# Gate matrices from three bfloat16 matmuls per token instead of one float32 matmul

## The chip, the cores and the metric

One core of a Trainium2 chip runs one step of a decoder layer for a prompt group (512 tokens) and a sample group (8 sequences of 4 tokens). The metric is the device time of one execution in microseconds. Runs of this kernel agree within about 0.5%.

## The reference, cut to what matters

The change lies in the last part of the layer, PEER: each token picks, for each of 8 heads, the 16 best of 128 x 128 one-neuron experts, and adds their outputs, weighted by a gate.

```
s1, i1 = lax.top_k(s[:, :, 0], PEER_TOPK)
s2, i2 = lax.top_k(s[:, :, 1], PEER_TOPK)
cand = (s1[..., :, None] + s2[..., None, :]).reshape(...)
cidx = (i1[..., :, None] * PEER_NKEYS + i2[..., None, :]).reshape(...)
top, pos = lax.top_k(cand, PEER_TOPK)
eidx = jnp.take_along_axis(cidx, pos, axis=-1)
gate = jax.nn.softmax(top, axis=-1)
a = jnp.einsum('thkd,td->thk', u_tab[eidx], xb).astype(jnp.float32)
act = (jax.nn.gelu(a) * gate).astype(xb.dtype)
return jnp.einsum('thk,thkd->td', act, v_tab[eidx])
```

An expert has a first index (0 to 127) and a second one (0 to 127). A token has 128 picks (8 heads of 16).

## The kernel before, in words

The first 384 prompt tokens are computed densely: all 128 x 128 experts for each token. The table of the first layer of experts, `u`, comes in 128 tiles of 128 experts x 1024; the second table, `v`, in another 128 tiles. Each tile is split into a rounded part `tHi` (ScalarE, `t_hi`) and a rest `tLo` (GpSimd, `lo_part`), and `product(n)` on TensorE is 24 matmuls of 128 x 384 over the tile and the split activations. The other tokens (the last 128 of the prompt and the 32 samples) are computed sparsely: `gather(q)` on GpSimd starts an indirect DMA of 128 rows of the table, and VectorE forms a dot product (`dot`, later `row_add`) against the activations in PSUM (`h_rows`).

The dense way needs, for each token, a 128 x 128 matrix of gates: zero but at the token's picks. It is built by TensorE as a product of two one-hot matrices. For one token, partition p is one of the 128 picks; `oh2` holds 1 where the second index of the pick is the column, `oh1` holds 1 where the first index is, and `w1` is `oh1` times the gate of the pick. `oh2` transposed times `w1` is the gate matrix. All are float32.

Work is cut into 48 steps of 8 tokens. `one_hots(st)` on VectorE (L1726) makes the matrices of a step by three instructions of 128 x 1024; `gate_product(st)` on TensorE (L926) multiplies them in two parts of four tokens, each part into one PSUM bank; ScalarE copies each part out to `stage` (L1251) and stores it to DRAM. Two buffers hold `oh2` and `w1`, so VectorE may be one step and a bit ahead: `one_hots(st)` waits for the products of step st - 2. The iota of the keys (`iota_p`) and the gates (`g_cols`) lie in PSUM, the indices (`idx12`) and `oh1` in SBUF.

The order on each engine is written out by hand. The 48 steps are laid over 62 table tiles, n = 51 to 112 (`gate_steps`): TensorE runs product(n) and behind it, for 48 of the 62, one gate_product. VectorE runs for each step `one_hots` and then two `dot`s. GpSimd runs `lo_part(n)` and then the gathers that are due (two for a step). ScalarE runs for each n the gelu of the product, `t_hi(n + 3)`, the store, and the two copies of a gate step. The stretch ahead of it on VectorE (L1694 to L1718) is the retrieval of the picks, four passes of `retrieve`, beside products 0 to 50 on TensorE.

Of the kernel before, what the change touches and what calls it, by code (L numbers as in the profile page):

```python
# [7 lines left out]
BF16 = mybir.dt.bfloat16  # L8
U32 = mybir.dt.uint32
ALU = mybir.AluOpType  # L10
# [3 lines left out]
P = 128  # L14
# [12 lines left out]
PH, PK = 8, 16  # L27
# [29 lines left out]
TD = T - P - TS  # L57
STILES = [TD, 0, 128, 256]
NST = len(STILES)
# [3 lines left out]
STEP_TOK = TB // 4  # L63
# [11 lines left out]
GATE_BANKS = (4, 5, 7)  # L75
# [60 lines left out]
def build(nc, a, o):  # L136
    with ExitStack() as ctx:
# [3 lines left out]
        def at(name, shape, offset, dt=F32):  # L141
            n = 4
            for s in shape[1:]:
                n *= s
            assert base <= offset and offset + n <= top and offset % 32 == 0, (name, offset, n)
            return nc.alloc_sbuf_tensor_at(name, shape, dt, offset=offset)
# [18 lines left out]
        iota = keep("iota", [P, P])  # L165
# [7 lines left out]
        pos_sq = pos[0]  # L173
# [11 lines left out]
        SPL_AT = TAB_AT + 32768  # L185
# [68 lines left out]
        at_ = TAIL + 6 * 2176 + 256  # L254
# [24 lines left out]
        tLo = at("tLo", [P, SPL, KT, P], TAB_AT + 16384, F32R)  # L279
        ug = at("ug", [P, UG, D], SPL_AT)  # L280
        ga = [at(f"ga{i}", [P, TD], (SPL_AT + 24576, SPL_AT + 24576 + 4 * TD, pos_sq + 6528)[i]) for i in range(3)]
        idx12 = at("idx12", [P, 2, TD], SPL_AT + 27648)
        a_s = at("a_s", [P, NDOT], SPL_AT + 30720)
        act_s = at("act_s", [P, NDOT], SPL_AT + 31360)
        eidx = at("eidx", [P, NDOT], SPL_AT + 32000, U32)
# [3 lines left out]
        zp = [Z_AT]  # L289

        def peer(name, shape, dt=F32):
            n = 4
            for q in shape[1:]:
                n *= q
            t = at(name, shape, zp[0], dt)
            zp[0] += -(-n // 32) * 32
            assert zp[0] <= C_AT + 26400, name
            return t
# [16 lines left out]

        zp[0] = Z_AT
        stage = peer("stage", [P, 2, NKEY, TB])
        oh2 = peer("oh2", [P, 2, STEP_TOK, P])
        w1 = peer("w1", [P, 2, STEP_TOK, P])
        oh1 = at("oh1", [P, STEP_TOK, P], pos_sq + 1024)  # L320

        zp[0] = Z_AT
        actHi0 = peer("actHi0", [P, GRP, TD], F32R)
# [14 lines left out]
        ps = ctx.enter_context(nc.psum_tensor("ps", [P, 8, 512], F32))  # L338
# [10 lines left out]

        flat = ps[:].rearrange("p b n -> p (b n)")  # L350
        h_rows = flat[:, 2 * 512:4 * 512]
        g_cols = flat[:, 6 * 512:6 * 512 + TD]
        iota_p = flat[:, 6 * 512 + TD:7 * 512]
        y_rows = h_rows

        def late_bank(n):
# [101 lines left out]
        s_oh = sem("one_hots_ready")  # L458
# [36 lines left out]
        def over(ap, n):  # L495

            return ap.unsqueeze(len(ap.shape)).broadcast_to(list(ap.shape) + [n])
# [171 lines left out]
        def _(pe):  # L669
            mm = nc.tensor.matmul  # L670
# [80 lines left out]
            for n in range(1, U_CONV):  # L751
# [7 lines left out]
                if n == 13:  # L759
# [5 lines left out]
                    for w, src in enumerate((row_r, row_li)):  # L765
                        for i in range(NH + 1):
                            m = P if i < NH else TS
                            c = 160 + (w * (NH + 1) + i) * NH
                            last = nc.tensor.transpose(ps[0:m, 6, c:c + NH], src[0:NH, i * P:i * P + m], ident[0:NH, 0:NH])
# [39 lines left out]
            for h in range(NH):  # L809
# [27 lines left out]
                for i in range(NH):  # L837
                    mm(ps[:, 6, i * P:TP], vtok[:, i, :], er[:, EOFF[i]:EOFF[i] + TP - i * P],
                       start=(i == 0), stop=(i == NH - 1))
                pe.wait_ge(s_c0, 16 * (h + 1))  # L840
                pe.wait_ge(s_qn, 1)
                for b in range(NB):
                    mm(ps[:, 2, 256 + b * NL:256 + (b + 1) * NL], csb[:, b, :], qwi[:, h, b * NL:(b + 1) * NL],
                       start=(b == 0), stop=False)
# [4 lines left out]
                for i in range(NH):  # L849
                    mm(ps[0:GR, 7, i * P:TP], dsel[:, h, :], er[:, EOFF[i]:EOFF[i] + TP - i * P],  # L850
                       start=(h == 0 and i == 0), stop=(h == NH - 1 and i == NH - 1))
# [74 lines left out]
            def gate_product(st):  # L926

                pe.wait_ge(s_oh, st + 1)
                for part in range(2):
                    i = 2 * st + part  # L930
                    if i >= len(GATE_BANKS):
                        pe.wait_ge(s_gev, i - len(GATE_BANKS) + 1)
                    for t in range(4):
                        last = mm(ps[:, GATE_BANKS[i % 3], t * P:(t + 1) * P], oh2[:, st % 2, 4 * part + t, :],  # L934
                                  w1[:, st % 2, 4 * part + t, :], start=True, stop=True)
                    last.then_inc(s_gmm, 1)

            for n in range(NCH):
# [6 lines left out]
                if n == N_SHUF:  # L945
                    pe.wait_ge(s_best, 1)
                    for q in range(3):
                        for i in range(1, NST):
                            last = nc.tensor.transpose(ps[:, 4 + q, (i - 1) * P:i * P], best[:, q, i, :], ident[:])
# [7 lines left out]
            for n in range(NCH, NT):  # L957
# [8 lines left out]
                if n == N_FOLD:  # L966
                    pe.wait_ge(s_yb, 1)
                    pe.wait_ge(s_flush, n - NCH - 1)
                    for k in range(KT):
                        last = mm(ps[:, late_bank(n + 2), k * TS:(k + 1) * TS], y_b[:, k * P:(k + 1) * P], fold[:],  # L970
                                  start=True, stop=True)
                    last.then_inc(s_fold, 1)
                if n == N_YT:
                    pe.wait_ge(s_yrow, 1)
                    for k in range(KT):
                        last = nc.tensor.transpose(y_rows[:, k * P:(k + 1) * P], ug[:, 0, k * P:(k + 1) * P], ident[:])
# [309 lines left out]
        def _(v):  # L1286
            link = linker(v, s_dch)
# [431 lines left out]
            v.wait_ge(s_bestT, 1)  # L1719
            for q in range(2):  # L1720
                nc.vector.tensor_copy(idx12[:, q], ps[:, 5 + q, 0:TD])
            link(nc.vector.tensor_copy(oh1[:, 0:4, :], ps[:, 4, :].rearrange("p (t c) -> p t c", c=P)))
            nc.vector.tensor_copy(iota_p, iota[:])
            link(nc.vector.tensor_copy(g_cols[:], oh1[:, 0:3, :].rearrange("p t c -> p (t c)")))

            def one_hots(st):  # L1726

                at_ = slice(STEP_TOK * st, STEP_TOK * (st + 1))
                keys_ = iota_p.unsqueeze(1).broadcast_to([P, STEP_TOK, P])
                if st >= 2:  # L1730
                    v.wait_ge(s_gmm, 2 * (st - 1))
                tt(oh2[:, st % 2], keys_, over(idx12[:, 1, at_], P), ALU.is_equal)
                if st:
                    v.wait_ge(s_oh, st)
                link(tt(oh1[:], keys_, over(idx12[:, 0, at_], P), ALU.is_equal))
                tt(w1[:, st % 2], oh1[:], over(g_cols[:, at_], P), ALU.mult).then_inc(s_oh, 1)

            for st in range(NSTEP):
                one_hots(st)
# [142 lines left out]
```

## Time and profile before

| what | us |
|---|---|
| median of 3 runs | 1723.83 (1715.46 to 1724.01) |
| the profiled execution, its own time | 1713.92 |
| its span, first to last instruction | 1712.2 |
| TensorE busy | 1670.4 (98%) |
| VectorE busy | 1183.7 (69%) |
| GpSimd busy | 1123.3 (66%) |
| ScalarE busy | 665.1 (39%) |
| granted TensorE clock, mean | 0.993 |

The span is the time from the first to the last instruction of the profiled execution. Durations are those of single instructions; neighbouring matmuls overlap in their pipeline, so the pace of a run of matmuls is read from the distance of their starts, not from their durations. The gate steps run from 750.7 us to 1089.3 us of the span.

### The profile page before, as it was taken

What the parts mean: (1) busy time and instruction counts of PE and PEld (TensorE: products, weight loads), DVE (VectorE), ACT (ScalarE), POOL (GpSimd) and SP (SyncE); (2) the same over time, 40 slices, a digit from 0 to 9 for tenths busy, and PEclk for the clock granted to TensorE, in tenths of its full rate; (3) what the DMA queues carried; (4) which work ended last, traced back from release to release, by engine and by line L of the source; (5) the groups of instructions that cost most, each with busy time, mean ns of one, the idle gap of its engine ahead of it and who ended that gap; (6) DMA issues with size and microseconds to landing.
All of it is one profiled execution on the core that took longest, in us unless ns stands there. A gap on an engine that the chain in (4) does not pass through costs nothing.

```text
span 1712.2 us, 27326 instructions
## 1 busy us (share of the span) xinstructions
PE 1670.4 (98%) x10559; PEld 1604.4 (94%) x10559; DVE 1183.7 (69%) x2324; ACT 665.1 (39%) x1059; POOL 1123.3 (66%) x677
## 2 busy tenths in 40 slices
PE   8999999899999999999999999999999999999996
PEld 3899878697999999999999999999999999999995
DVE  4340244645777899999787778446787888888755
ACT  2554222333334333343433433334444344444442
POOL 1767322132336888877766676778889799999952
PEclk9999999999999999999999999999999999999998
DMA  8645222044204999979999999979999999999951
GB/s 280 213 154 160 74 72 101 13 143 148 89 36 141 308 299 295 341 260 337 351 342 349 347 352 339 340 300 352 394 406 405 362 408 401 407 407 400 401 187 62
DMA packets 192705, 461.27 MB, mean 269 GB/s; under 512 B 21184, under 2 KB 99008, under 8 KB 192448
## 3 DMA queue, kind: packets, MB, share of 16 engines
q1 hardware_dynamic: 79872, 242.31, 40.3%
q0 software_dynamic: 46080, 167.79, 26.0%
q10 hardware_dynamic: 66624, 49.42, 8.7%
q8 instruction: 84, 1.38, 0.3%
q14 instruction: 45, 0.37, 0.1%
HBM read 407.64 MB, written 51.83 MB: 268 GB/s over the span
## 4 chain that ended last, share of the span: by engine, by line
PE 54%; DVE 4%; issue 1%; POOL 0%; DVEq 0%; ACT 0%
PE ps L923 49%; PE ps L934 5%; DVE ug L1575 1%; DVE yo L1821 0%; DVE eqb L1687 0%; DVE rs L1819 0%; DVE pick L1674 0%; DVE ps L1585 0%; POOL tLo L649 0%; DVE cand L1652 0%; DVE rs L1297 0%; PE ps L676 0%; DVE pos L1660 0%; DVE eqa L1678 0%; DVE pos L1651 0%
## 5 line engine op out<-in xcount | busy, mean ns | idle before, releaser
L649 POOL TENSOR_TENSOR tLo<-tab,tHi 128x1024 fp32r<-128x1024 f32 x256 | 621.4, 2428 | 163.5 <-ACT tHi L1174 160.6
L1174 ACT CAST tHi<-tab 128x1024 fp32r<-128x1024 f32 x256 | 268.1, 1047 | 288.0 <-PE ps L923 219.7
L923 PE MATMUL ps<-hHi,tLo 128*128 128x384 f32 x1024 | 352.1, 344 | 0.0
L923 PE MATMUL ps<-hHi,tHi 128*128 128x384 f32 x1024 | 345.7, 338 | 0.0
L923 PE MATMUL ps<-hLo,tHi 128*128 128x384 f32 x1024 | 344.9, 337 | 0.0
L923 PE MATMUL ps<-actHi,tLo 128*128 128x384 f32 x1024 | 342.5, 334 | 1.6 <-POOL tLo L649 1.6
L923 PE MATMUL ps<-actLo,tHi 128*128 128x384 f32 x1024 | 342.2, 334 | 0.0
L923 PE MATMUL ps<-actHi,tHi 128*128 128x384 f32 x1024 | 342.2, 334 | 0.0
L637 POOL TENSOR_TENSOR wLo<-raw,wHi 128x1024 fp32r<-128x1024 f32 x53 | 128.0, 2416 | 289.6 <-ACT wHi L1005 289.6
L1575 DVE SCALAR_TENSOR_TENSOR ug<-ug,ps 128x1024 f32<-128x1024 f32 x160 | 191.4, 1217 | 46.8 <-DMA ug<-in_urows,eidx 45.7
L1585 DVE SCALAR_TENSOR_TENSOR ps<-ug,act_s,ps 128x1024 f32<-128x1024 f32 x158 | 202.5, 1282 | 5.0
L923 PEld LDWEIGHTS ps<-actHi,tLo 128*128 128x128 f32 x1024 | 192.2, 188 | 2.1 <-issue 1.9
L923 PEld LDWEIGHTS ps<-hHi,tHi 128*128 128x128 f32 x1024 | 193.2, 189 | 0.0
L923 PEld LDWEIGHTS ps<-hHi,tLo 128*128 128x128 f32 x1024 | 193.2, 189 | 0.0
L923 PEld LDWEIGHTS ps<-hLo,tHi 128*128 128x128 f32 x1024 | 192.6, 188 | 0.0
L923 PEld LDWEIGHTS ps<-actHi,tHi 128*128 128x128 f32 x1024 | 192.2, 188 | 0.0
L923 PEld LDWEIGHTS ps<-actLo,tHi 128*128 128x128 f32 x1024 | 192.2, 188 | 0.0
L1235 ACT ACTIVATE ga<-ps 128x384 f32<-128x384 f32 x112 | 54.9, 490 | 351.5 <-PE ps L923 351.5
L693 PE MATMUL ps<-hHi,wLo 128*128 128x272 f32 x848 | 180.0, 294 | 7.4 <-DVEq L1460 2.8
L659 POOL DMA_INDIRECT ug<-in_urows,eidx x160 | 158.4, 990 | 38.1 <-issue 27.6
L659 POOL DMA_INDIRECT ug<-in_vrows,eidx x160 | 151.4, 947 | 43.3 <-issue 22.7
L693 PE MATMUL ps<-hLo,wHi 128*128 128x272 f32 x848 | 175.7, 289 | 0.0
(356 smaller groups left out, 2471.8 us busy)
## 6 DMA issues: line engine op xcount, KB each, us to landing
tab<-in_tab SPq DMA_DIRECT2D x256, 512.0 KB, 6.6
raw<-in_w SPq DMA_DIRECT2D x101, 512.0 KB, 4.2
gate_scratch<-stage ACTq DMA_DIRECT2D x48, 512.0 KB, 6.4
gt<-gate_scratch SPq DMA_DIRECT2D x32, 768.0 KB, 6.9
gelu_scratch<-ga ACTq DMA_DIRECT2D x112, 192.0 KB, 5.9
gin<-gelu_scratch SPq DMA_DIRECT2D x112, 192.0 KB, 9.6
ug<-in_urows,eidx POOLq DMA_INDIRECT x160, 6.8
ug<-in_vrows,eidx POOLq DMA_INDIRECT x160, 7.6
```

The lines of the kernel that those rows point to most:

```text
L637: pool.tensor_tensor(wLo[:, i % 2], raw[:, p % RAW], wHi[:, i % 2].bitcast(F32), ALU.subtract).then_inc(s_wlo, 1)
L649: pool.tensor_tensor(tLo[:, n % SPL], tab[:, n % TABS], tHi[:, n % SPL].bitcast(F32), ALU.subtract).then_inc(s_tlo, 1)
L659: pool.indirect_dma_start(ug[:, q % UG, :], None, a["urows"] if q < NDOT else a["vrows"], bass.IndirectOffsetOnAxis(ap=eidx[:, q % NDOT:q ...
L693: last = mm(pair(n)[:, h], w, x[:, k, h * HF:(h + 1) * HF], start=first, stop=end)
L923: last = mm(ps[:, bank, 0:TD], w, x[:, k, 0:TD], start=first, stop=end)
L934: last = mm(ps[:, GATE_BANKS[i % 3], t * P:(t + 1) * P], oh2[:, st % 2, 4 * part + t, :], w1[:, st % 2, 4 * part + t, :], start=True, stop ...
L1174: nc.scalar.copy(tHi[:, n % SPL], tab[:, n % TABS]).then_inc(s_thi, 1)
L1235: f(out, ps[:, n % 2, 0:TD], ACT.Gelu_apprx_tanh).then_inc(s_gelu, 1)
L1575: stt(ug[:, slot], ug[:, slot], 1.0, h_rows, ALU.mult, ALU.mult, accum_out=a_s[:, q:q + 1]).then_inc(s_item, 1)
L1585: stt(y_rows, ug[:, slot], act_s[:, k:k + 1], y_rows, ALU.mult, ALU.add).then_inc(s_item, 1)
```

## The change

The one-hots, the indices, the iota and the gates become bfloat16. An index up to 127 and a 0 or 1 are exact in bfloat16; a gate is split into three bfloat16 pieces (`gate3`: rounded, the rest rounded, the rest of that), and for each token three matmuls, one per piece, are added up in PSUM. The pieces are made once, ahead of the steps. In the tiles two tokens are interleaved: the last dimension is a pair of tokens, so an operand that repeats along the keys still has two neighbouring elements. TensorE reads one token of a pair, with a step of two elements. The iota (`key2`) and the gates no longer lie in PSUM: every operand of the step's VectorE instructions is in SBUF.

```diff
+        oh2 = at("oh2", [P, 2, STEP_TOK // 2, P, 2], zp[0], BF16)
+        w3 = at("w3", [P, 2, 3, STEP_TOK // 2, P, 2], zp[0] + 4096, BF16)
+        oh1 = at("oh1", [P, STEP_TOK // 2, P, 2], pos_sq + 512, BF16)
+        key2 = at("key2", [P, P, 2], pos_sq + 512 + 2048, BF16)
+        idx12 = at("idx12", [P, 2, TD], pos_sq + 512 + 4096, BF16)
...
-        g_cols = flat[:, 6 * 512:6 * 512 + TD]
-        iota_p = flat[:, 6 * 512 + TD:7 * 512]
...
                     for t in range(4):
-                        last = mm(ps[:, GATE_BANKS[i % 3], t * P:(t + 1) * P], oh2[:, st % 2, 4 * part + t, :],
-                                  w1[:, st % 2, 4 * part + t, :], start=True, stop=True)
+                        out, pair_, one = ps[:, GATE_BANKS[i % 3], t * P:(t + 1) * P], 2 * part + t // 2, t % 2
+                        keys_, pieces = oh2[:, st % 2, pair_, :, one], w3[:, st % 2, :, pair_, :, one]
+                        for piece in range(3):
+                            last = mm(out, keys_, pieces[:, piece], start=(piece == 0), stop=(piece == 2))
...
-            link(nc.vector.tensor_copy(oh1[:, 0:4, :], ps[:, 4, :].rearrange("p (t c) -> p t c", c=P)))
-            nc.vector.tensor_copy(iota_p, iota[:])
-            link(nc.vector.tensor_copy(g_cols[:], oh1[:, 0:3, :].rearrange("p t c -> p (t c)")))
+            nc.vector.tensor_copy(key2[:], over(iota[:], 2))
+            link(nc.vector.tensor_copy(gate3[:, 0], ps[:, 4, 0:TD]))
+            link(tt(gate_rest[:], ps[:, 4, 0:TD], gate3[:, 0], ALU.subtract))
+            link(nc.vector.tensor_copy(gate3[:, 1], gate_rest[:]))
+            link(tt(gate_rest[:], gate_rest[:], gate3[:, 1], ALU.subtract))
+            link(nc.vector.tensor_copy(gate3[:, 2], gate_rest[:]))
 
             def one_hots(st):
 
                 at_ = slice(STEP_TOK * st, STEP_TOK * (st + 1))
-                keys_ = iota_p.unsqueeze(1).broadcast_to([P, STEP_TOK, P])
+                keys_ = key2[:].unsqueeze(1).broadcast_to([P, STEP_TOK // 2, P, 2])
+
+                def along_keys(of_tokens):
+
+                    pairs_ = of_tokens.rearrange("p (q two) -> p q two", two=2)
+                    return pairs_.unsqueeze(2).broadcast_to([P, STEP_TOK // 2, P, 2])
+
                 if st >= 2:
                     v.wait_ge(s_gmm, 2 * (st - 1))
-                tt(oh2[:, st % 2], keys_, over(idx12[:, 1, at_], P), ALU.is_equal)
+                tt(oh2[:, st % 2], keys_, along_keys(idx12[:, 1, at_]), ALU.is_equal)
                 if st:
                     v.wait_ge(s_oh, st)
-                link(tt(oh1[:], keys_, over(idx12[:, 0, at_], P), ALU.is_equal))
-                tt(w1[:, st % 2], oh1[:], over(g_cols[:, at_], P), ALU.mult).then_inc(s_oh, 1)
+                link(tt(oh1[:], keys_, along_keys(idx12[:, 0, at_]), ALU.is_equal))
+                for piece in range(3):
+                    last = tt(w3[:, st % 2, piece], oh1[:], along_keys(gate3[:, piece, at_]), ALU.mult)
+                last.then_inc(s_oh, 1)
```

On VectorE, from the end of the retrieval to the first dots of the first step, this stands in the kernel before (`idx_137` is `idx12`, `oh_159` is `oh2`, `oh_161` is `oh1`, `w_160` is `w1`, `ps` is PSUM):

```order
L1721 COPY idx_137<-ps 128x384 x2
L1722 COPY oh_161<-ps 128x512
L1723 COPY ps<-iota 128x128
L1724 COPY ps<-oh_161 128x384
L1732 TENSOR_TENSOR oh_159<-ps,idx_137 128x1024
L1735 TENSOR_TENSOR oh_161<-ps,idx_137 128x1024
L1736 TENSOR_TENSOR w_160<-oh_161,ps 128x1024
L1575 SCALAR_TENSOR_TENSOR ug,a_s<-ug,ps 128x1024 x2
```

and this in the changed one (`key_163` is `key2`, `oh_160` is `oh2`, `oh_162` is `oh1`, `w_161` is `w3`, `gate_137` is `gate3`):

```order
L1725 CAST idx_164<-ps 128x384 x2
L1726 CAST key_163<-iota 128x256
L1727 CAST gate_137<-ps 128x384
L1728 TENSOR_TENSOR gate_rest<-ps,gate_137 128x384
L1729 CAST gate_137<-gate_rest 128x384
L1730 TENSOR_TENSOR gate_rest<-gate_rest,gate_137 128x384
L1731 CAST gate_137<-gate_rest 128x384
L1745 TENSOR_TENSOR oh_160<-key_163,idx_164 128x1024
L1748 TENSOR_TENSOR oh_162<-key_163,idx_164 128x1024
L1750 TENSOR_TENSOR w_161<-oh_162,gate_137 128x1024 x3
L1579 SCALAR_TENSOR_TENSOR ug,a_s<-ug,ps 128x1024 x2
```

The place of the dots is the same; ahead of the first step stand 8 small instructions where 5 stood, and in every step 5 instructions of 128 x 1024 where 3 stood. The three of before have one SBUF input each, the five have two.

On TensorE, behind product(51), one part of a gate step between matmuls of the products stands in the kernel before as

```order
L923 MATMUL ps<-hLo,tHi 128x384
L934 MATMUL ps<-w_160,oh_159 128x128 x8
L923 MATMUL ps<-hHi,tLo 128x384
```

and in the changed one as

```order
L925 MATMUL ps<-hLo,tHi 128x384
L939 MATMUL ps<-w_161,oh_160 128x128 x24
L925 MATMUL ps<-hHi,tLo 128x384
```

One row here is a whole step of 8 tokens: 8 matmuls before, 24 now, at the same place between the products. (The trace shows a float32 matmul as two records.) GpSimd's and ScalarE's orders are the same in both.

## Rows read from the trace of the kernel before

**Rows 1.** The page: busy time of the engines; the chain that ended last.

```profile
PE 1670.4 (98%) x10559; PEld 1604.4 (94%) x10559; DVE 1183.7 (69%) x2324; ACT 665.1 (39%) x1059; POOL 1123.3 (66%) x677
...
PE ps L923 49%; PE ps L934 5%; DVE ug L1575 1%; DVE yo L1821 0%; DVE eqb L1687 0%; DVE rs L1819 0%; DVE pick L1674 0%; DVE ps L1585 0%; POOL tLo L649 0%; DVE cand L1652 0%; DVE rs L1297 0%; PE ps L676 0%; DVE pos L1660 0%; DVE eqa L1678 0%; DVE pos L1651 0%
```

**Rows 2.** Windows inside the gate stage: busy us by engine, clock, DMA share, GB/s.

```profile
900.00:950.00 50.00, 50.00 (x327) 50.00 (x327) 40.11 (x48) 19.73 (x32) 34.42 (x23) 1.00 1.02 353
```

**Rows 3.** Line 934, the gate matmuls: durations min/median/max, starts; who waited for them.

```profile
L934 PE MATMUL ps<-w,oh x768: 271/275/377, 750.7 to 1089.3; 128*128 128x128 f32 x192
...
  DVE oh L1732: 46.4, 12
```

**Rows 4.** Timeline of TensorE, one gate step and one product: start, duration, engine, line.

```profile
901.94 1.93 PEld L934 LDWEIGHTS ps<-w,oh 128*128 128x128 f32 x16
...
903.78 0.19 PEld L923 LDWEIGHTS ps<-hHi,tLo 128*128 128x128 f32 x1
...
907.94 0.19 PEld L934 LDWEIGHTS ps<-w,oh 128*128 128x128 f32 x1
```

**Rows 5.** Timeline of TensorE: sixteen 128-column matmuls with one pass each, merged.

```profile
538.08 1.90 PE L911 MATMUL ps<-identR,h_b 128*128 128x128 f32 x16
```

**Rows 6.** Timeline of VectorE, one gate step: first one-hot, first dot, next step.

```profile
904.09 1.22 DVE L1732 TENSOR_TENSOR oh<-ps,idx 128x1024 f32<-128x1024 f32 x1 [4.18 <-PE ps L934]
...
907.62 1.21 DVE L1575 SCALAR_TENSOR_TENSOR ug<-ug,ps 128x1024 f32<-128x1024 f32 x1
...
910.09 1.22 DVE L1732 TENSOR_TENSOR oh<-ps,idx 128x1024 f32<-128x1024 f32 x1
```

**Rows 7.** Timeline of VectorE in the retrieval, instructions with two SBUF inputs.

```profile
716.99 3.27 DVE L1674 TENSOR_TENSOR pick<-pabf,pcut 128x128 bf16<-128x128 f32 x1
...
732.61 0.69 DVE L1687 TENSOR_TENSOR eqa<-eqa 128x1024 bf16<-128x1024 bf16 x1
733.22 0.69 DVE L1687 TENSOR_TENSOR eqb<-eqb 128x1024 bf16<-128x1024 bf16 x1
733.94 0.42 DVE L1687 TENSOR_TENSOR eqa<-eqa 128x512 bf16<-128x512 bf16 x1
```

**Rows 8.** Timeline of GpSimd around the first row of Rows 7.

```profile
716.57 1.00 POOL L659 DMA_INDIRECT ug<-in_urows,eidx  x1 [0.30 <-issue]
717.60 2.41 POOL L649 TENSOR_TENSOR tLo<-tab,tHi 128x1024 fp32r<-128x1024 f32 x1
```

**Rows 9.** VectorE groups, 537 to 750 us (retrieval): shapes, count, busy us, mean ns, idle.

```profile
L1682 DVE TENSOR_TENSOR eqa<-eqa,ixt 128x2048 bf16<-128x2048 bf16 x4 | 13.3, 3314 | 0.1
L1678 DVE TENSOR_TENSOR eqa<-ranks,pick 128x2048 bf16<-128x2048 bf16 x4 | 7.8, 1940 | 0.0
L1687 DVE TENSOR_TENSOR eqb<-eqb 128x256 bf16<-128x256 bf16 x5 | 7.2, 1432 | 0.0
L1674 DVE TENSOR_TENSOR pick<-pabf,pcut 128x128 bf16<-128x128 f32 x4 | 6.7, 1664 | 0.0
L1687 DVE TENSOR_TENSOR eqb<-eqb 128x512 bf16<-128x512 bf16 x4 | 6.1, 1522 | 0.0
L1687 DVE TENSOR_TENSOR eqa<-eqa 128x1024 bf16<-128x1024 bf16 x4 | 5.6, 1394 | 0.0
...
L1682 DVE TENSOR_TENSOR eqb<-eqb,ixt 128x2048 bf16<-128x2048 bf16 x4 | 4.8, 1211 | 0.0
...
L1687 DVE TENSOR_TENSOR eqa<-eqa 128x512 bf16<-128x512 bf16 x4 | 1.7, 424 | 0.1
...
L1687 DVE TENSOR_TENSOR eqa<-eqa 128x256 bf16<-128x256 bf16 x5 | 1.5, 292 | 0.2
```

**Rows 10.** Groups of the gate stage, 745 to 1095 us, same columns.

```profile
L649 POOL TENSOR_TENSOR tLo<-tab,tHi 128x1024 fp32r<-128x1024 f32 x62 | 149.1, 2405 | 85.3 <-ACT tHi L1174 85.2
L1575 DVE SCALAR_TENSOR_TENSOR ug<-ug,ps 128x1024 f32<-128x1024 f32 x98 | 116.7, 1216 | 13.8 <-DMA ug<-in_urows,eidx 13.6
...
L1721 DVE COPY idx<-ps 128x384 f32<-128x384 f32 x2 | 1.0, 552 | 1.3 <-PE ps L949 1.3
```

More of the change, by code:

```diff
@@ L281, in build @@
         ga = [at(f"ga{i}", [P, TD], (SPL_AT + 24576, SPL_AT + 24576 + 4 * TD, pos_sq + 6528)[i]) for i in range(3)]
-        idx12 = at("idx12", [P, 2, TD], SPL_AT + 27648)
+        gate3 = at("gate3", [P, 3, TD], SPL_AT + 27648, BF16)
         a_s = at("a_s", [P, NDOT], SPL_AT + 30720)
@@ L317, in build @@
         stage = peer("stage", [P, 2, NKEY, TB])
-        oh2 = peer("oh2", [P, 2, STEP_TOK, P])
-        w1 = peer("w1", [P, 2, STEP_TOK, P])
-        oh1 = at("oh1", [P, STEP_TOK, P], pos_sq + 1024)
+        gate_rest = at("gate_rest", [P, TD], zp[0])
+        oh2 = at("oh2", [P, 2, STEP_TOK // 2, P, 2], zp[0], BF16)
[3 more added lines that the diff above has]
+        idx12 = at("idx12", [P, 2, TD], pos_sq + 512 + 4096, BF16)
+        assert 512 + 4096 + 4 * TD <= 3 * NST * PH * PK * 4
         zp[0] = Z_AT
```

## The prediction

> **What bounds the kernel now.** I read the page first: TensorE is busy for 98% of the span, and the chain that ended last runs over it, 49% through the products of the tables and 5% through the gate matmuls [rows 1]. 5% of 1712.2 is 86 us: that is all that cheaper gate matmuls could give if nothing took their place. The windows of the gate stage show TensorE without a gap at full clock, while VectorE is busy for 40 us of 50 and GpSimd for 34 [rows 2]; the DMA share is already about 1, so I also ask below what transfers do. The rows on the gate line say how close VectorE is: it waited for TensorE 12 times in 48 steps, 46.4 us together [rows 3]; in the other steps it arrived about when it was needed. So the stage has one bound and a second engine right behind it, and each is costed for itself.
>
> **TensorE, per step.** The weight loads give the pace: a gate step of 8 tokens begins at 901.94, the next product at 903.78, the next gate step at 907.94 [rows 4]. A gate step is 1.84 us (88 us for 48), a product 4.16 us, that is 0.173 us for each of its 24 matmuls of 384 columns. The stage of 62 products and 48 gate steps is 62 x 4.16 + 48 x 1.84 = 346 us, so TensorE needs 7.21 us for each gate step with its share of products (62/48 = 1.29 products, 5.37 us).
>
> After, a step is 24 bfloat16 matmuls of 128 columns. The trace has none. From below: 128 columns at the products' pace per column, 0.173 x 128/384 = 0.058 us. From above: sixteen matmuls of 128 columns in one pass take 1.90 us from first start to last end, about 0.11 us from start to start once the last one's duration of 0.27 is taken off [rows 5]; their weights are 4-byte and are loaded anew for each, so they may be paced by the load. Bfloat16 weights are half as many bytes; I take 0.065, near the lower end, since the products' row is the one in which columns and not loads set the pace. The ends for 1152 matmuls are 67 and 127 us, the value 75: against 88 that is -21, +39 and -13 us. TensorE would then need 5.37 + 24 x 0.065 = 6.93 us for a step.
>
> The Trainium skill ("TensorE: Matmul & The Clock Gate", section "Back-to-back issue gap") gives about 81 ns for each load-and-matmul pair at 128 columns in a sustained stream. By that the matmuls would take 93 us and TensorE alone would be 5 us slower than before; no row here shows a bfloat16 pair.
>
> **VectorE, per step.** Before: three instructions from 904.09 to 907.62, 3.53 us, then two dots with their accumulator reads until 910.09, 2.47 us, in all 6.0 us [rows 6]. To this come waits for gathered rows, 13.6 us over the stage [rows 10], 0.28 a step. After: five bfloat16 instructions of 1024. In the retrieval such instructions start 0.61 us apart, and 0.72 where the chain is linked [rows 7]; four by 0.61 and one by 0.72 is 3.16 us. The operand that repeats along the keys changes slowly but its innermost two elements are neighbours; L1682, whose second operand repeats too with eight neighbours inside, takes 1.21 us for 2048 [rows 9], the same rate, so I take it for granted here. Alone the change of type gives 0.37 us a step back: three instructions became five. Sum: 3.16 + 2.47 + 0.28 = 5.91 us, below TensorE's 6.93.
>
> But all five now have both inputs in SBUF, where before one input of each lay in PSUM. The retrieval shows what such instructions meet. A 128-element subtraction started at 716.99 lasts 3.27 us [rows 7]; GpSimd was in a gather from 716.57 to 717.57 and in a `tLo` subtraction from 717.60 to 720.01, and VectorE's instruction ended 0.25 us behind that [rows 8]. The f32 one-hots of before, beside the same `tLo`, show nothing of the kind: 1.22 us each [rows 6]. I conclude that a VectorE instruction with two SBUF inputs stands still while GpSimd's subtraction runs.
>
> The Trainium skill ("SBUF — State Buffer", section "Who interferes with whom") says it as a rule: a VectorE instruction with two SBUF inputs contends with a GpSimd instruction that reads SBUF, and the later one waits for all of the other. By that rule VectorE becomes the bound of the stage; without it TensorE stays the bound and the sum is -13 us. The two rows at 717 us agree with it.
>
> The size, from the groups of the retrieval [rows 9], for one pass: the two of 2048 that stall, (3.31 - 1.21) + (1.94 - 1.21) = 2.8 us; 1024, 1.39 - 0.69 = 0.7; 512, 1.52 - 0.42 = 1.1; 256, (1.43 - 0.29) x 5/4 = 1.4; the 128 pick, 1.66 less about 0.27, 1.4. Together 7.5 us of standing on 7.9 us of work (four 2048 at 1.21, two each at 0.69, 0.42, 0.29, one at 0.27), 0.94 us per us. There a `tLo` came every 4.16 us. In the gate stage one comes 1.29 times a step; with a step of about 8 us that is every 6.2 us, so the ratio is 0.94 x 4.16/6.2 = 0.63, and 3.16 us of work stand for 2.0 us. Bounds: all of the 1.29 `tLo` of 2.41 us [rows 10] and half a microsecond for each of two gathers, 4.1 us; and nothing, if the dots, which read PSUM and can run beside GpSimd, happen to cover each `tLo`.
>
> A step is then 5.91 + 2.0 = 7.9 us on VectorE against 6.93 on TensorE: TensorE waits for the one-hots, the stage lasts 48 x 7.9 = 380 us, +33 us against 346. Queued behind a standing one-hot are the two dots and with them the slots of the gathers, but these have three steps of room. GpSimd in turn waits at most one VectorE instruction (0.6 us) for each of its own, and has 35% of the stage idle [rows 2]. DMA carries the same bytes in a longer stage, so its share of about 1 falls and costs nothing; it would matter only if the stage became shorter.
>
> **Ahead of the steps.** Five small instructions become eight, of about 0.55 us by the row of a 384 copy [rows 10]: some +2 us, with a link between most, less 0.4 us on the first three one-hots; one has two SBUF inputs and may stand. TensorE waits there already, so +2 us is on the path.
>
> **Sum.** +33 + 2 = +35 us on the profiled execution's 1713.9 us: 1749 us, with its span at 1747. That execution stands 10 us under the median of the three runs; half of this for where a new median will lie gives 1754 us.
>
> **The rivals.**
> (B) *TensorE stays the bound.* VectorE's standing is below 1.0 us a step, because the dots cover it. For it: dots and accumulator reads are 2.47 us, as long as one `tLo`. Against: in the retrieval dots lie between too, and the stalls came all the same. Then -13 + 2 = -11 us: 1703, with the same 5 us for the median 1708 (1700 if a matmul takes 0.058).
> (C) *The new matmuls are paced by their weight load*, 0.11 us each: TensorE needs 5.37 + 2.66 = 8.0 us a step and is at least level with VectorE: +39 + 2, 1760 us. For it: [rows 5]; against: half the bytes.
> (D) *The change doesn't do what it says on VectorE*: with only pairs inside, the instructions run at the float32 rate, 5 x 1.18 = 5.9 us, a step is 8.6 us without and 12 with standing (0.63 of 5.9 is 3.7): +67 to over +200 us. Against: L1682.
>
> **How the numbers follow.** A 0.60, B 0.20, C 0.12, D 0.08. A's own range is a standing of 1.2 to 3.1 us, steps of 7.1 to 9.0 us: -5 to +86, that is 1716 to 1807 us. The whole range takes in the upper half of B and leaves out most of D: 1706 to 1806. What a measurement can tell from no change is about 0.5%, 9 us. Faster: 0.15 of B and 0.07 at A's low end, 0.22. Same: 0.05 of B, 0.05 of A, 0.10. Slower: 0.48 of A, C and D, 0.68.
>
> **What would show it.** In the trace of the changed kernel: the five one-hot instructions with a mean well above 0.69 us and a maximum near 3 us, long ones ending just behind a `tLo`; TensorE idle ahead of the gate matmuls, released by the last product with the gates, about 1 us a step; the gate line's first to last start some 370 us apart instead of 339; matmul starts 0.06 to 0.07 us apart. Wrong would be: one-hots all at 0.69 us (no standing, B), TensorE without gaps and the matmuls at 0.11 (C), or a minimum of 1.2 us for the one-hots (D).

## The result, and the profile after

The changed kernel takes 1729.43 us (median of 14 runs, 1725.46 to 1738.45) against 1722.51 us of the kernel before (14 runs, 1715.16 to 1726.48, a spread of 0.7% where 0.5% is said above): a ratio of 1.0058, 95% interval 1.0038 to 1.0078. It is slower by about 10 us, or 0.6%. The forecast was slower by 30. Its profiled execution took 1736.84 us with a span of 1735.1 us, 22.9 us more than the span of before; about half of that lies ahead of all that was changed, as shown below.

On the page of the changed kernel, the engines and the chain:

```profile
PE 1664.7 (96%) x10943; PEld 1587.8 (92%) x10943; DVE 1264.5 (73%) x2423; ACT 668.6 (39%) x1059; POOL 1144.0 (66%) x677
...
PE 34%; DVE 24%; issue 1%; POOL 0%; DVEq 0%; ACT 0%
PE ps L925 34%; DVE w L1750 7%; DVE ug L1579 7%; DVE oh L1745 5%; DVE oh L1748 2%; DVE yo L1836 0%; DVE eqb L1691 0%; DVE rs L1834 0%; DVE eqb L1686 0%; DVE ixt L1644 0%; DVE ps L1589 0%; DVE eqa L1682 0%; DVE pcut L1673 0%; POOL tLo L651 0%; DVE key L1726 0%
```

The gate matmuls are gone from the chain [rows 1]; in their place VectorE has 24% of it, with the one-hots (L1745, L1748, L1750) and the dots (L1579). A window of the gate stage, the counterpart of [rows 2], says the same: VectorE is full, TensorE no longer.

```profile
900.00:950.00 50.00, 47.12 (x368) 45.68 (x367) 49.79 (x58) 18.92 (x31) 38.26 (x23) 1.00 0.98 332
```

The gate line of the changed kernel: durations min/median/max, first and last start, and what TensorE waited for (us, times).

```profile
L939 PE MATMUL ps<-w,oh x1152: 217/218/308, 764.9 to 1111.9; 128*128 128x128 bf16 x192
its engine sat idle before it (us, times) until:
  DVE w L1750: 56.6, 41
```

and who waited for the products with the gates (L1750):

```profile
  PEld ps L939: 31.6, 26
  PE ps L939: 25.0, 15
```

From first to last start the stage lasts 347.0 us; in [rows 3] it is 1089.3 - 750.7 = 338.6 us. Before, VectorE waited for TensorE 12 times; now TensorE waits for VectorE. The 56.6 us and 41 times of the gate line are the waits of the weight loads (31.6, 26) and of the matmuls (25.0, 15) added up, and mostly the same waits seen twice: at 808.69 us a load waits for 1.75 us, and at 808.70 its matmul for 1.44. TensorE's matmuls are kept waiting 25 us in the stage, about 0.5 us a step.

The groups of the stage, 745 to 1110 us (busy us, mean ns; the 128 x 1024 instructions of VectorE, and GpSimd's two):

```profile
L651 POOL TENSOR_TENSOR tLo<-tab,tHi 128x1024 fp32r<-128x1024 f32 x63 | 155.9, 2474 | 72.5 <-ACT tHi L1178 71.6
L1750 DVE TENSOR_TENSOR w<-oh,gate 128x1024 bf16<-128x1024 bf16 x144 | 124.1, 917 | 1.7
L1579 DVE SCALAR_TENSOR_TENSOR ug<-ug,ps 128x1024 f32<-128x1024 f32 x96 | 113.0, 1213 | 0.0
L661 POOL DMA_INDIRECT ug<-in_urows,eidx x98 | 108.7, 1109 | 29.2 <-issue 15.0 <-DVE ug L1579 9.1
...
L1745 DVE TENSOR_TENSOR oh<-key,idx 128x1024 bf16<-128x1024 bf16 x48 | 90.9, 1893 | 0.0
...
L1748 DVE TENSOR_TENSOR oh<-key,idx 128x1024 bf16<-128x1024 bf16 x48 | 32.6, 679 | 0.0
```

Undisturbed, one of the five takes 0.68 us. Where nothing stands (`psum5` below) the same three groups have 90.4, 33.1 and 32.7 us busy; here they have 124.1, 90.9 and 32.6. The difference, 33.7 + 57.8 - 0.1 = 91.4 us, is 1.9 us of standing a step: time in which an instruction is held up. (My expectations below say 1.75; that came from subtracting single durations, which overlap by 0.07 us where instructions follow one another.) The dots wait for no gathered row any more (0.0, where [rows 10] has 13.6 us).

VectorE and GpSimd side by side, two steps and a half of the changed kernel (start, duration):

```profile
890.53 2.56 DVE L1745 TENSOR_TENSOR oh<-key,idx 128x1024 bf16<-128x1024 bf16 x1
...
895.54 1.21 DVE L1579 SCALAR_TENSOR_TENSOR ug<-ug,ps 128x1024 f32<-128x1024 f32 x1
...
897.82 0.92 DVE L1745 TENSOR_TENSOR oh<-key,idx 128x1024 bf16<-128x1024 bf16 x1
...
899.38 4.11 DVE L1750 TENSOR_TENSOR w<-oh,gate 128x1024 bf16<-128x1024 bf16 x3
...
905.69 2.94 DVE L1745 TENSOR_TENSOR oh<-key,idx 128x1024 bf16<-128x1024 bf16 x1
```

```profile
890.13 2.42 POOL L651 TENSOR_TENSOR tLo<-tab,tHi 128x1024 fp32r<-128x1024 f32 x1 [2.19 <-ACT tHi L1178]
...
895.79 2.41 POOL L651 TENSOR_TENSOR tLo<-tab,tHi 128x1024 fp32r<-128x1024 f32 x1 [0.56 <-ACT tHi L1178]
900.00 2.94 POOL L651 TENSOR_TENSOR tLo<-tab,tHi 128x1024 fp32r<-128x1024 f32 x1 [1.80 <-ACT tHi L1178]
...
905.67 2.42 POOL L651 TENSOR_TENSOR tLo<-tab,tHi 128x1024 fp32r<-128x1024 f32 x1
```

The one-hot that starts at 890.53 ends 0.54 us behind the subtraction that runs until 892.55, a little less than an undisturbed one needs. The subtraction of 895.79 falls on the two dots (895.54 to 897.82) and costs 0.2 us. That of 900.00 is itself stretched to 2.94 us by the running product and then holds the next for over 2 us; that of 905.67 starts just before the one-hot and costs it 2.3 us. Of the four subtractions here the dots cover one.

**Where the profiled execution's 22.9 us lie.** The transposes of the picks start at 743.4 us before and at 754.5 us after: 11.1 us come ahead of all that was changed. In a second profile of the kernel before (experiment 6) they start at 751.6 us, so 8.2 of the 11.1 us come without the change too. TensorE's wait for VectorE at the second turn to the sparse tokens, in the changed kernel's trace:

```profile
700.15 0.48 PE L913 MATMUL ps<-identR,hHi 128*128 128x128 f32 x1 [5.75 <-DVE ug L1579]
```

and in that of before:

```profile
692.29 0.33 PE L911 MATMUL ps<-identR,hHi 128*128 128x128 f32 x1 [0.58 <-DVE ug L1575]
```

Behind the long wait the granted clock is 0.56 in the ten microseconds from 700 (1.00 before), so the products there run for most of them at the lower of its two levels, 1.2 instead of 2.4 GHz. From the transposes to the first gate matmul it is 10.4 us instead of 7.3 (+3.1), the stage is +8.4, what follows it 623.2 instead of 622.9 (+0.3). 11.1 + 3.1 + 8.4 + 0.3 = 22.9. The part from the transposes on, where the change lies, is 11.8 us, which fits the ratio.

### The profile page after: what moved, and what is told of

Read it like the earlier page. It is cut to its first block, busy times and chain, and to the rows that moved or that the text cites. A ratio compares the mean times of both kernels' runs of the same rounds, so it can differ in the third digit from the quotient of the medians.

```text
span 1735.1 us, 28193 instructions
## 1 busy us (share of the span) xinstructions
PE 1664.7 (96%) x10943; PEld 1587.8 (92%) x10943; DVE 1264.5 (73%) x2423; ACT 668.6 (39%) x1059; POOL 1144.0 (66%) x677
## 4 chain that ended last, share of the span: by engine, by line
PE 34%; DVE 24%; issue 1%; POOL 0%; DVEq 0%; ACT 0%
PE ps L925 34%; DVE w L1750 7%; DVE ug L1579 7%; DVE oh L1745 5%; DVE oh L1748 2%; DVE yo L1836 0%; DVE eqb L1691 0%; DVE rs L1834 0%; DVE eqb L1686 0%; DVE ixt L1644 0%; DVE ps L1589 0%; DVE eqa L1682 0%; DVE pcut L1673 0%; POOL tLo L651 0%; DVE key L1726 0%
## 5 line engine op out<-in xcount | busy, mean ns | idle before, releaser
L1579 DVE SCALAR_TENSOR_TENSOR ug<-ug,ps 128x1024 f32<-128x1024 f32 x160 | 190.1, 1216 | 35.6 <-DMA ug<-in_urows,eidx 34.6
L661 POOL DMA_INDIRECT ug<-in_urows,eidx x160 | 174.4, 1090 | 44.1 <-issue 23.4
L695 PE MATMUL ps<-hHi,wHi 128*128 128x272 f32 x848 | 176.4, 289 | 0.0
```

The source lines that it names most:

```text
L661: pool.indirect_dma_start(ug[:, q % UG, :], None, a["urows"] if q < NDOT else a["vrows"], bass.IndirectOffsetOnAxis(ap=eidx[:, q % NDOT:q ...
L695: last = mm(pair(n)[:, h], w, x[:, k, h * HF:(h + 1) * HF], start=first, stop=end)
L1579: stt(ug[:, slot], ug[:, slot], 1.0, h_rows, ALU.mult, ALU.mult, accum_out=a_s[:, q:q + 1]).then_inc(s_item, 1)
```

## The experiments

The measure of each is the stage, first to last start of the gate matmuls (338.6 before, 347.0 after), and its ratio to the kernel before.

**1. GpSimd's subtraction cut short.**

```diff
+                q = slice(0, 8 if 53 <= n < 115 else P)
+                k = slice(0, 1 if 53 <= n < 115 else KT)
-            pool.tensor_tensor(tLo[:, n % SPL], tab[:, n % TABS], ...
+                pool.tensor_tensor(tLo[:, n % SPL, k, q], tab[:, n % TABS, k, q], ...
```

> The changed kernel with GpSimd's tLo subtraction cut from 128x1024 to 128x8 for tiles 53 to 114 (the rest of tLo is left as it was, so that part of the products is left out); gathers, DMAs and all waits stay. Theory (VectorE's one-hots stand still while GpSimd's subtraction holds the SBUF read they share): the five one-hot instructions fall from means of 1.9, 0.68 and 0.86 us to about 0.7 to 0.8, VectorE's step from 7.4 to about 5.9 us, TensorE becomes the bound, and the gate matmuls' first to last start takes about 322 us instead of 347 (61 products at 4.16 and 47 steps at 1.45). Rival 1 (the gathers hold it, not the subtraction): the one-hot means stay above 1.2 us and the stage near 345. Rival 2 (VectorE isn't the bound of the stage): one-hots get short, the stage stays at 347.

Its groups on VectorE, 745 to 1120 us, and its gate line:

```profile
L1752 DVE TENSOR_TENSOR w<-oh,gate 128x1024 bf16<-128x1024 bf16 x144 | 91.0, 686 | 1.6
L1747 DVE TENSOR_TENSOR oh<-key,idx 128x1024 bf16<-128x1024 bf16 x48 | 33.1, 690 | 46.8 <-PE ps L941 45.0
L1750 DVE TENSOR_TENSOR oh<-key,idx 128x1024 bf16<-128x1024 bf16 x48 | 33.1, 690 | 0.0
```

```profile
L941 PE MATMUL ps<-w,oh x1152: 217/218/233, 753.6 to 1075.7; 128*128 128x128 bf16 x192
```

No one-hot or product stands any more (the longest takes 0.694 us), VectorE waits for TensorE again, and the stage takes 322.1 us; 1700.11 us, ratio 0.9873 (0.9825 to 0.9921). The gathers were all there, so they don't hold a one-hot up: rival 1 is out, and with it the half microsecond for each gather in my upper bound.

**2. TensorE with one piece, VectorE with three.**

```diff
-                        for piece in range(3):
-                            last = mm(out, keys_, pieces[:, piece], start=(piece == 0), stop=(piece == 2))
+                        for piece in range(1):
+                            last = mm(out, keys_, pieces[:, piece], start=True, stop=True)
```

> The changed kernel with TensorE multiplying only the first of the three pieces (8 bfloat16 matmuls a step instead of 24; the other two pieces are left out of the product); VectorE makes all three as before. Theory (VectorE bounds the stage): first to last start of the gate matmuls stays at 345 to 350 us, and the 0.9 us that TensorE saves in each step comes back as idle time ahead of the gate matmuls (57 us becomes about 100). Rival (the matmul stream or TensorE's turn-round sets the pace): the stage shrinks by up to 47 x 0.92 = 43 us, to about 304.

```profile
L939 PE MATMUL ps<-w,oh x384: 217/218/308, 755.2 to 1113.9; 128*128 128x128 bf16 x192
its engine sat idle before it (us, times) until:
  DVE w L1750: 128.9, 57
```

With two thirds of the gate matmuls gone the stage is longer, 358.7 us; ratio 1.0098 (1.0060 to 1.0136). VectorE bounds it. (The 128.9 us count loads and matmuls again; the matmuls alone wait for 59.8 us.) That it grew by 12 us I had not expected. TensorE is idle for longer, and the clock that it is granted is 0.89 to 0.97 in the windows of 50 us from 800 us on, against 1.00 in the changed kernel. But VectorE is busy for 49.8 us of each 50 in both, so the lower clock doesn't lengthen the stage by itself; the 12 us are on VectorE. Its groups:

```profile
L1750 DVE TENSOR_TENSOR w<-oh,gate 128x1024 bf16<-128x1024 bf16 x144 | 155.5, 1134 | 1.7
...
L1745 DVE TENSOR_TENSOR oh<-key,idx 128x1024 bf16<-128x1024 bf16 x48 | 65.4, 1362 | 0.0
L1748 DVE TENSOR_TENSOR oh<-key,idx 128x1024 bf16<-128x1024 bf16 x48 | 39.2, 818 | 0.0
```

By the same subtraction 104 us of standing in place of 91, and now more of it in the products than in the first one-hot: the same subtractions of GpSimd fall on other instructions, and cost 2.2 us a step instead of 1.9.

**3. VectorE with one piece, TensorE with three products.**

```diff
-                            last = mm(out, keys_, pieces[:, piece], start=(piece == 0), stop=(piece == 2))
+                            last = mm(out, keys_, pieces[:, 0], start=(piece == 0), stop=(piece == 2))
...
-                for piece in range(3):
+                for piece in range(1):
                     last = tt(w3[:, st % 2, piece], ...
```

> The changed kernel with VectorE multiplying only the first piece of the gates (3 instructions of 128x1024 a step instead of 5); TensorE still runs 24 matmuls a step, all on that piece. Theory: VectorE's step falls to about 4.4 us and at most 1.2 us of standing, TensorE becomes the bound without gaps, the stage takes about 322 us (this is the case in which the change would have gained 16 us in the stage). Rival (bfloat16 matmuls with a step of two elements, or the copies out on ScalarE, hold the stage): it stays above 335 us.

```profile
L939 PE MATMUL ps<-w,oh x1152: 217/218/233, 754.4 to 1077.7; 128*128 128x128 bf16 x192
...
  issue: 7.2, 45
  DVE w L1750: 7.0, 5
```

The stage takes 323.3 us, ratio 0.9893 (0.9844 to 0.9942). All 1152 bfloat16 matmuls are there: on TensorE the change does what it is meant to. The standing missed its expectation: the two one-hots and the one product have 75.7, 62.0 and 35.7 us busy, by the same subtraction 1.6 us a step where at most 1.2 was expected. VectorE has room for it here, so the stage doesn't show it. Three such instructions stand for 1.6 us, five for 1.9.

**4. The kernel before, with both operands in SBUF.**

```diff
-                keys_ = iota_p.unsqueeze(1).broadcast_to([P, STEP_TOK, P])
+                keys_ = iota[:].unsqueeze(1).broadcast_to([P, STEP_TOK, P])
...
-                tt(w1[:, st % 2], oh1[:], over(g_cols[:, at_], P), ALU.mult).then_inc(s_oh, 1)
+                tt(w1[:, st % 2], oh1[:], over(g_sb[:, at_], P), ALU.mult).then_inc(s_oh, 1)
```

> The kernel before, float32 and one matmul per token, with the iota of the keys and the gates read from SBUF instead of PSUM: each of the three one-hot instructions has two SBUF inputs. Theory (the place of the operands, not the type, brings the standing): the three rise from 1.22 us to means between 1.4 and 2.4, VectorE's step from 6.0 to 7.3 to 7.8 us against TensorE's 7.21, the stage from 339 to between 343 and 365 us, the kernel 0.2 to 1.5% slower than before. Rival (the standing belongs to bfloat16 at the packed rate): all stays at 1.22 us and 339 us.

```profile
L1731 DVE TENSOR_TENSOR oh<-iota,idx 128x1024 f32<-128x1024 f32 x48 | 89.8, 1871 | 0.0
L1734 DVE TENSOR_TENSOR oh<-iota,idx 128x1024 f32<-128x1024 f32 x48 | 86.9, 1810 | 0.0
L1735 DVE TENSOR_TENSOR w<-oh,g_sb 128x1024 f32<-128x1024 f32 x47 | 86.8, 1846 | 1.6
```

```profile
L935 PE MATMUL ps<-w,oh x768: 271/275/422, 760.9 to 1123.6; 128*128 128x128 f32 x192
```

The three go from 1.22 us to 1.81 to 1.87, the stage from 338.6 to 362.7 us, ratio 1.0113 (1.0071 to 1.0156). The standing comes with the place of the operands and not with the type: 1.8 us a step here, with float32.

**5. Operands back in PSUM.** The pieces and the iota are made in SBUF and copied once to PSUM as 4-byte words, two bfloat16 each. `psum4` has room for the iota and two pieces:

```diff
+        in_ps = flat[:, 6 * 512:7 * 512].bitcast(BF16)
+        key_ps = in_ps[:, 0:2 * P].rearrange("p (k two) -> p k two", two=2)
+        gate_ps = in_ps[:, 2 * P:2 * P + 2 * TD].rearrange("p (g t) -> p g t", g=2)
...
-                    last = tt(w3[:, st % 2, piece], oh1[:], along_keys(gate3[:, piece, at_]), ALU.mult)
+                    last = tt(w3[:, st % 2, piece], oh1[:], along_keys(gate_ps[:, piece, at_] if piece < 2 else gate3[:, 2, at_]), ALU.mult)
```

> The changed kernel with the doubled iota and the first two gate pieces read from PSUM (copied there once, 4-byte words that hold two bfloat16 each), so that four of the five one-hot instructions of a step have one SBUF input; only the third product has two. Theory (two SBUF inputs are the cause): the four stand no longer (0.69 us), the fifth keeps a mean of 0.9 to 1.5 us; a step on VectorE needs about 6.1 us, TensorE bounds the stage, 322 to 326 us, the kernel 0.5 to 1.2% faster than before. Rival (bfloat16 from PSUM doesn't run at the packed rate): the four take 1.2 us each, a step 8 us, the stage over 380 us.

`psum5` also frees a gate bank for the rest:

```diff
-GATE_BANKS = (4, 5, 7)
+GATE_BANKS = (4, 5)
...
+        key_ps = ps[:, 7, 0:P].bitcast(BF16).rearrange("p (k two) -> p k two", two=2)
+        in_ps = flat[:, 6 * 512:7 * 512].bitcast(BF16)
+        rest_ps = ps[:, 7, P:P + 64].bitcast(BF16)
...
-                    last = tt(w3[:, st % 2, piece], oh1[:], along_keys(gate3[:, piece, at_]), ALU.mult)
+                    last = tt(w3[:, st % 2, piece], oh1[:], along_keys(gate_ps(piece, st)), ALU.mult)
```

> As psum4, but all five one-hot instructions read one operand from PSUM: the gate matmuls use two banks in turn instead of three, the third piece and the iota lie in the freed one; the doubled iota is also made ahead of the retrieval instead of right ahead of the steps. Theory: no standing in the stage, all five at 0.69 us, stage 322 us, and 2 us less ahead of it; 0.8 to 1.4% faster than before. Rival (three banks are needed, because the copies out on ScalarE come late): TensorE idles ahead of the gate matmuls for 0.5 us or more a step, the stage is 340 us or more.

Groups of `psum5`, 745 to 1090 us, and one gate step on TensorE's weight loads:

```profile
L663 POOL TENSOR_TENSOR tLo<-tab,tHi 128x1024 fp32r<-128x1024 f32 x64 | 154.5, 2413 | 71.2 <-ACT tHi L1190 71.1
...
L673 POOL DMA_INDIRECT ug<-in_urows,eidx x97 | 91.6, 944 | 28.8 <-issue 17.9 <-DVE ug L1591 7.2
L1766 DVE TENSOR_TENSOR w<-oh,ps 128x1024 bf16<-128x1024 bf16 x144 | 90.4, 683 | 1.7
...
L1761 DVE TENSOR_TENSOR oh<-ps,idx 128x1024 bf16<-128x1024 bf16 x48 | 33.1, 690 | 33.3 <-PE ps L951 33.2
L1764 DVE TENSOR_TENSOR oh<-ps,idx 128x1024 bf16<-128x1024 bf16 x48 | 32.7, 681 | 0.0
```

```profile
905.39 1.38 PEld L951 LDWEIGHTS ps<-w,oh 128*128 128x128 bf16 x24 [0.16 <-issue]
906.73 0.19 PEld L937 LDWEIGHTS ps<-hHi,tLo 128*128 128x128 f32 x1
```

With the full subtractions in place nothing stands, and bfloat16 from PSUM runs at the packed rate. The stage takes 323.7 us in `psum5` (754.0 to 1077.7) and 323.6 in `psum4` (763.8 to 1087.4), where the fifth instruction has a median of 0.685 us and a maximum of 1.88 us. Its mean is 0.77 us, below the 0.9 to 1.5 expected: one instruction with two SBUF inputs stands for 0.09 us a step, far less than a fifth of 1.9. Over all: `psum4` 1704.9 us, ratio 0.9931 (0.9904 to 0.9959); `psum5` 1706.0 us, 0.9921 (0.9899 to 0.9942). Both beat both kernels, by 0.7 to 0.8% the one before and by about 1.3% the changed one: the change pays once its operands are where the old ones were. Between the two no difference can be told. Two banks are enough: in `psum5` TensorE's loads idle 0.16 us ahead of a gate step, not the 0.5 of the rival. Ahead of the steps `psum5` takes 9.9 us from the transposes to the first gate matmul, 0.5 less than the changed kernel and not 2: three copies to PSUM were added, and a conversion of the gates stands there (1.12 us for 0.36).

**6. The iota made early; the kernel before once more.**

```diff
             nc.vector.tensor_copy(identR[:], ident[:]).then_inc(s_idr, 1)
+            nc.vector.tensor_copy(key2[:], over(iota[:], 2))
...
-            nc.vector.tensor_copy(key2[:], over(iota[:], 2))
             link(nc.vector.tensor_copy(gate3[:, 0], ps[:, 4, 0:TD]))
```

> The changed kernel with only one edit: the doubled iota is made ahead of the retrieval, so its 2.4 us conversion no longer stands between the transposed picks and the first one-hots. Theory: from the transposes to the first gate matmul 8.2 us instead of 10.4, TensorE's idle time there 4.9 to 2.7 us, stage unchanged at 345 to 350 us; in all 2 to 4 us less than the changed kernel, ratio to before 1.002 to 1.006. Rival (this wait costs nothing because VectorE bounds what follows anyway): the stage starts 2 us earlier but lasts 2 us longer.

The row that it takes away, in the changed kernel:

```profile
756.70 2.42 DVE L1726 CAST key<-iota 128x256 bf16<-128x256 f32 x1
```

From the transposes to the first gate matmul it is 8.9 us (10.4 with the row; 8.2 expected), the stage 347.0. The gain of 1.5 us is there in the trace; the ratio of 1.0068 (1.0044 to 1.0092; 1.002 to 1.006 expected) cannot show it.

Why the conversion takes 2.42 us, though it has a single SBUF input, can be read off the traces. In the changed kernel GpSimd's subtraction runs beside it; in experiment 1 (second fence) the subtraction is already the short one at this place:

```profile
756.54 2.41 POOL L651 TENSOR_TENSOR tLo<-tab,tHi 128x1024 fp32r<-128x1024 f32 x1
```

```profile
747.26 0.21 POOL L653 TENSOR_TENSOR tLo<-tab,tHi 128x8 fp32r<-128x8 f32 x1
...
747.51 0.28 DVE L1728 CAST key<-iota 128x256 bf16<-128x256 f32 x1
```

The same conversion takes 0.28 us without the long subtraction; with it, it ends 0.17 us behind the subtraction's end at 758.95. So 2.1 of the 2.42 us are standing. The iota moved away, the next conversion from SBUF to SBUF stands in its place (early_key):

```profile
756.00 1.04 DVE L1730 CAST gate<-gate_rest 128x384 bf16<-128x384 f32 x1
```

It takes 0.36 us in the changed kernel. The 0.7 us more is what is missing of the expected 2.2 us. The kernel before copied the iota from SBUF to PSUM in 0.29 us (at 746.28), inside a subtraction from 745.42 to 747.80; undisturbed such a copy takes 0.30 (`psum5`, at 749.7). That copy does not stand.

> The kernel before once more, unchanged, for a second profile of it. Theory: stage 338.6 us again within 1 us and 7.3 us from the transposes to the first gate matmul; what differs from execution to execution is how long TensorE waits for VectorE at the second turn to the sparse tokens near 693 us (0.6 us or 5.8 us, depending on how GpSimd's subtractions fall on VectorE's retrieval). Rival: the stage itself varies by 5 us or more.

```profile
L934 PE MATMUL ps<-w,oh x768: 271/275/378, 759.4 to 1098.0; 128*128 128x128 f32 x192
```

```profile
698.44 0.47 PE L911 MATMUL ps<-identR,hHi 128*128 128x128 f32 x1 [5.75 <-DVE ug L1575]
```

The stage of the kernel before is 338.6 us a second time, to the tenth, and the long wait of 5.75 us is there without the change, as the expectation has it. The ratio is 1.0006 (0.9980 to 1.0032), as it should be. Of the twelve traces of this study six have the wait of 0.6 us and six one of 5.6 to 6.6 us, on kernels whose code up to there is the same but for `split_tlo` and the early iota.

**7. The same instructions in another order.** First dot of a step between the one-hots and the products:

```diff
                 link(tt(oh1[:], keys_, along_keys(idx12[:, 0, at_]), ALU.is_equal))
+                sparse(L2_DOTS[-1] + 2 * st + 1)
                 for piece in range(3):
```

> The changed kernel with the first dot of each step moved between the two one-hots and the three products with the gate pieces (same instructions, other order). Theory (the standing is set by where GpSimd's subtraction falls in VectorE's cycle, so its mean is no constant of the instruction count): the standing per step leaves 1.75 us; with two windows of 1.2 us instead of one of 2.5 us no subtraction of 2.4 us can be covered whole, so I expect 2.0 to 2.6 us, a stage of 357 to 385 us. Rival (the standing depends only on how many two-input instructions and subtractions there are, as I forecast it from the retrieval): 1.75 us and 345 to 350 us again.

```profile
L939 PE MATMUL ps<-w,oh x1152: 217/218/308, 758.3 to 1121.4; 128*128 128x128 bf16 x192
```

The stage takes 363.1 us, ratio 1.0187 (1.0138 to 1.0236), with 2.2 us of standing a step by the same subtraction (busy 120.0, 90.8 and 52.5 us). The rival is out: the standing is not set by the count of instructions alone.

**8. GpSimd's subtraction in two halves.**

```diff
+                for k in (slice(0, 4), slice(4, KT)):
+                    last = pool.tensor_tensor(tLo[:, n % SPL, k], tab[:, n % TABS, k], tHi[:, n % SPL, k].bitcast(F32), ALU.subtract)
```

> The changed kernel with each of GpSimd's subtractions issued as two halves of 128x512, back to back. Theory (an instruction is held off for the whole of the other engine's one): a VectorE instruction stands for at most one half at a time, about 1.25 us, and passes between the halves if the share is handed over in turn: maximum of a one-hot about 2.0 us instead of 3.3, standing per step 1.2 to 1.8 us, stage 325 to 347 us; the longer GpSimd chain costs nothing. Rival (GpSimd's next instruction gets in first, as behind the gather at 717 us): the maximum stays at 3.2 us or more and the stage at 345 us or more.

```profile
L1752 DVE TENSOR_TENSOR w<-oh,gate x144: 677/686/3425, 761.7 to 1107.5; 128x1024 bf16<-128x1024 bf16 x144
```

The longest product takes 3.4 us (3.3 without the split), so the second half can get in ahead of a waiting VectorE instruction, as the rival has it: at 943.52 us three products take 4.63 us instead of 1.90, over two halves that run back to back from 945.05 to 947.60. In other steps VectorE passes between the halves (a one-hot of 1.04 us at 889.66). The standing is 1.9 us a step (busy 131.5, 66.9 and 48.0 us) and the stage 345.9 us: as good as unchanged. Ratio 1.0101 (1.0071 to 1.0131), no gain; this run's trace is one with the long wait.

## Why the prediction was wrong, step by step

**The mechanism (case A) held.** Two SBUF inputs, GpSimd's subtraction, VectorE as the bound, long instructions up to 3.3 us: in experiments 1, 3, 4 and 5 the stage goes where the theory puts it; in experiment 2 VectorE is the bound as forecast, but the stage came out 9 us longer than the expected range. TensorE's wait was forecast at about 1 us a step and is 0.5 (25 us in 48 steps), because VectorE's step is shorter than forecast. One reading was too generous: at 716.99 us VectorE's instruction had started 0.6 us ahead of the subtraction of 717.60 and still ended behind it [rows 7, rows 8]. The rows show the standing, but not that the later one is the one that waits, as the rule quoted beside them has it.

**TensorE's 6.93 us a step was right.** A gate step's 24 loads start over 1.34 us (905.39 to 906.73), 0.056 us each, at the lower end rather than the 0.065 I took and far from the 0.081 that the prediction quotes; 0.16 us a step, in which the loads idle ahead of a gate step, makes up for most of it. Where TensorE bounds the stage it takes 322 to 324 us; 47 steps of 6.89.

**VectorE's 7.9 us a step was too much.** The stage has 347.0/47 = 7.38 us a step. Term by term:

| term of a step | forecast | measured | from |
|---|---|---|---|
| five one-hot instructions | 3.16 | 3.14 | 893.01 to 895.54, and 0.61 for the first |
| two dots | 2.47 | 2.28 | 895.54 to 897.82 |
| waits for gathered rows | 0.28 | 0.0 | idle of L1579 |
| standing | 2.0 | 1.9 | busy against `psum5` |
| sum | 7.9 | 7.3 | |

The start of L1748 at 893.01 is in the trace between the rows shown above. The standing, the term that no row of before could show, was within 5%. That it was so near is in part luck. The rule behind it (0.94 us for each us of work when a subtraction comes every 4.16 us) was used with a step of 8 us; with the step that came, 7.38 us, it gives 0.94 x 4.16/5.7 x 3.16 = 2.2 us. And for the one instruction with two SBUF inputs of `psum4` it gives nearly 0.5 us, where 0.09 were measured. What failed are the two terms that I read straight off the trace. The waits for gathered rows were there because VectorE came early; once it is the late one, the rows have landed. And the 2.47 us of the dots ran to the start of the next one-hot [rows 6], with about 0.2 us in it in which VectorE waited for TensorE: the one-hot of 910.09 starts 2.15 us behind the first load of a gate step (907.94), as the one of 904.09 does, which is on record as released by TensorE (901.94 and 904.09 [rows 4, rows 6]). Both are waits of an engine with room, and I carried them over to an engine without. Together 0.47 us of the 0.53; times 48 that is 23 us of a stage for which the forecast difference was 33.

The step that failed is thus "a step is then 5.91 + 2.0 = 7.9 us", and in it the 5.91. The term that was mis-sized is the 2.47 + 0.28 of dots and waits: it measured 2.28. Made with 5.45 the forecast of the stage would have been 47 x 7.45 = 350 us, +12 instead of +33, where +8.4 was measured. The forecast was the difference of two numbers near 350, so 6% in one of them is two thirds of the result.

**How far the standing can be known.** The same subtractions beside the same five instructions stand for 1.9, 2.2 and 2.2 us a step (changed kernel, experiments 2 and 7). That is some 15 us of the stage, more than the 8.4 us by which the change lengthened it.

**Ahead of the steps** +2 us was forecast and +3.1 measured; 2.42 us of it is the conversion of the iota, which I priced at 0.55 like its neighbours; 2.1 us of that is standing (experiment 6). The prediction's rule names instructions with two SBUF inputs only, and this one has a single one: the rule was too narrow.

**Rivals.** B was wrong as to the cover by the dots (one of the four subtractions in the stretch shown), C and D by the rows (0.056 us a matmul; 0.68 us a one-hot, with only pairs inside).

## What to carry to other kernels

Before an operand is moved, ask which memory the other operand is in and who else reads there: the same new type took 15 us off a stage of 339 with one operand in PSUM, and added 8 with both in SBUF beside GpSimd. Where an engine with room becomes the bound, cost its step from starts between which it waited for nothing, without the waits that its room let it have. And where a forecast is the difference of two long stages, a few per cent in one of them can be most of the result.

## What the runs showed of the hardware that I had not expected

- The hold is on one side only for gathers: a one-hot never stands for one (0.694 us at most beside all gathers in experiment 1), but the gathers' instructions on GpSimd grow from a mean of 0.944 us before to 1.109 beside one-hots with two SBUF inputs, and are back at 0.944 in `psum5`.
- A conversion from SBUF to SBUF, with a single input, stands beside GpSimd's subtraction (2.42 us for 0.28, 1.04 for 0.36), a float32 copy from SBUF to PSUM does not (0.29 us; all in experiment 6).
- Removing work from TensorE made the stage longer (experiment 2, 347 to 359 us), with more standing (2.2 us a step for 1.9) and a lower granted clock. That a shift of GpSimd's subtractions against VectorE's cycle is behind it is my reading; experiment 7 shows that order alone can do as much.
- Bfloat16 matmuls of 128 columns with a load of weights ahead of each, both operands read with a step of two elements, go at 0.056 us each; one-pass matmuls with 4-byte operands of the same size at 0.11 [rows 5].
- VectorE reads pairs of bfloat16 in PSUM, brought there by a copy of 4-byte words, at 0.68 us for 1024 elements, as from SBUF. That every bit of the second and third piece arrives is not shown by these runs.
